# Expert tokens turned by VectorE in 32x32 blocks instead of by TensorE

## The reference, cut to what matters

```
aff = softmax(tok @ router_w)                 # (512, 16), per sequence
gate, idx = top_k(aff.T, 64)                  # per expert
xs = tok[idx]                                 # 128 slots of both sequences x 1024
hid = silu(xs @ w_gate[e]) * (xs @ w_up[e])   # 1024 -> 1408
ye = (hid @ w_down[e]) * gate                 # 1408 -> 1024
out = zeros.at[idx].add(ye)
```

## Time and profile before

| what | us |
|---|---|
| median of three runs | 1491.75 |
| span of the profiled execution, first to last instruction | 1489.4 |
| TensorE busy | 1467.0 |
| VectorE busy | 1189.5 |
| ScalarE busy | 819.8 |
| GpSimd busy | 167.3 |

### The profile page before, as it was taken

One profiled execution on the slowest core, in us unless ns is written; L12 is line 12 of the kernel. 1 busy time (PEld: TensorE's weight loads), 2 busy tenths in 40 slices (PEclk: granted clock), 3 DMA queues, 4 the chain that ended last, 5 costly groups with the idle time before them and its releaser, 6 DMA issues.

```text
span 1489.4 us, 18913 instructions
## 1 busy us (share of the span) xinstructions
PE 1467.0 (99%) x7042; PEld 1235.5 (83%) x7042; DVE 1189.5 (80%) x1024; ACT 819.8 (55%) x777; POOL 167.3 (11%) x119
## 2 busy tenths in 40 slices
PE   9999999999999999998999999999999999999996
PEld 8878888888888888888888888888888888888885
DVE  5688988896767766346888888888888888888886
ACT  6322232123622222333677777777777777777776
POOL 1000001000005200011110112011110121012101
PEclk9999999999999999999999999999999999999998
DMA  7210232623263255677999999999999999999997
GB/s 236 58 43 0 81 87 75 224 85 99 94 230 121 87 183 197 227 253 283 347 362 365 376 376 374 384 374 377 374 377 381 377 374 374 384 376 376 374 374 286
DMA packets 220971, 388.26 MB, mean 261 GB/s; under 512 B 8603, under 2 KB 87771, under 8 KB 220412
## 3 DMA queue, kind: packets, MB, share of 16 engines
q1 hardware_dynamic: 213692, 361.39, 68.4%
q0 software_dynamic: 7232, 26.22, 5.8%
HBM read 348.78 MB, written 38.80 MB: 260 GB/s over the span
## 4 chain that ended last, share of the span: by engine, by line
PE 71%; DVE 2%; DMA 0%; issue 0%; ACT 0%; POOLq 0%; POOL 0%; ACTq 0%
PE ps L1779 23%; PE ps L1781 22%; PE ps L1780 22%; PE ps L2162 1%; PE ps L2154 1%; PE ps L2199 1%; PE ps L2082 0%; PE ps L2064 0%; DMA slot_tokens<-tok_rows,rows_to_gather 0%; DVE top_index L1651 0%; DVE affinity_rows L1654 0%; DVE top_of_halves L1647 0%; DVE expert_lo L1207 0%; DVE tok_rows L1592 0%; ACT expert_hi L804 0%
## 5 line engine op out<-in xcount | busy, mean ns | idle before, releaser
L1207 DVE TENSOR_TENSOR expert_lo<-expert_raw,expert_hi 128x2048 fp32r<-128x2048 f32 (+1 forms) x285 | 597.5, 2110 | 92.1 <-ACT expert_hi L804 91.1
L804 ACT ACTIVATE expert_hi<-expert_raw 128x2048 fp32r<-128x2048 f32 (+1 forms) x285 | 506.5, 1778 | 177.8 <-PE ps L1781 174.0
L1779 PE MATMUL ps<-expert_hi,slot_tokens_T_hi 128*128 128x512 f32 (+1 forms) x768 | 289.8, 377 | 2.0 <-DVE slot_tokens_T_lo L1207 1.0
L1780 PE MATMUL ps<-expert_lo,slot_tokens_T_hi 128*128 128x512 f32 (+1 forms) x768 | 285.2, 371 | 0.0
L1781 PE MATMUL ps<-expert_hi,slot_tokens_T_lo 128*128 128x512 f32 (+1 forms) x768 | 285.2, 371 | 0.0
L1779 PE MATMUL ps<-hT_hi,w_hi 128*128 128x512 f32 x576 | 226.2, 393 | 1.0 <-DVE hT_lo L1219 1.0
L1781 PE MATMUL ps<-hT_hi,w_lo 128*128 128x512 f32 x576 | 224.3, 389 | 0.0
L1780 PE MATMUL ps<-hT_lo,w_hi 128*128 128x512 f32 x576 | 224.2, 389 | 0.0
L1779 PEld LDWEIGHTS ps<-expert_hi,slot_tokens_T_hi 128*128 128x128 f32 x768 | 144.1, 188 | 25.1 <-issue 4.0
L1781 PEld LDWEIGHTS ps<-expert_hi,slot_tokens_T_lo 128*128 128x128 f32 x768 | 144.2, 188 | 20.4
L1241 DVE SCALAR_TENSOR_TENSOR conv_sum<-a_padded,small_params,conv_sum 128x1024 f32<-128x1024 f32 x120 | 158.1, 1317 | 3.4
(11 more groups left out here) (314 smaller groups left out, 1843.6 us busy)
## 6 DMA issues: line engine op xcount, KB each, us to landing
expert_raw<-in_w_gate SPq DMA_DIRECT2D x64, 1024.0 KB, 8.7
expert_raw<-in_w_up SPq DMA_DIRECT2D x64, 1024.0 KB, 8.6
expert_raw<-in_w_down SPq DMA_DIRECT2D x64, 1024.0 KB, 8.1
expert_raw<-in_w_gate SPq DMA_DIRECT2D x32, 768.0 KB, 7.5
expert_raw<-in_w_up SPq DMA_DIRECT2D x32, 768.0 KB, 7.2
expert_raw<-in_w_down SPq DMA_DIRECT2D x32, 768.0 KB, 8.5
w_raw<-in_w_in SPq DMA_DIRECT2D x36, 512.0 KB, 4.8
gate_in<-gate_spill SPq DMA_DIRECT2D x22, 512.0 KB, 3.9
```

The costliest lines, as they stand in the source:

```text
L804: nc.scalar.activation(out, src, ACT.Copy, **scale).then_inc(s, 1)
L1207: V.tensor_tensor(out, src, high_part.bitcast(F32), ALU.subtract).then_inc(s, 1)
L1779: nc.tensor.matmul(out, a[0], b[0], start=first, stop=False)
L1780: nc.tensor.matmul(out, a[0], b[1], start=False, stop=False)
```

## The change

VectorE turns the tokens of experts 1 to 15. It transposes 32x32 blocks only, and within a group of 32 partitions. So the tokens are gathered in another order: each slot's row of 1024 channels is cut into four pieces of 256 (1 KB), and partition group b gets piece b of the slots. Column group a of `slot_tokens` (256 columns) holds slots 32a to 32a + 31. That takes four gathers per expert, with a list of pieces (4 x row + quarter) that is made once: four small ScalarE copies, four small TensorE transposes (`slot_pieces`) and one VectorE operation. Read with a step of 8 elements (32 bytes) and turned block by block, the tokens come out with channel 8p + k on partition p of tile k, so the gate and up blocks are loaded with partition p holding rows 8p + 4kh to 8p + 4kh + 3. The w_down blocks are loaded as they were.

The turning (`turn_tokens`) is one VectorE instruction of 128 x 1024 elements into a buffer of its own (`turned_tokens`), at n = 8 of the body before. The split reads this buffer, not PSUM, and stands ahead of the split of block 0 on both ScalarE and VectorE. TensorE loses the eight transposes in all bodies but for expert 0; it does `hidden_T(2)` straight behind unit 17 and waits for the tokens' low part after it. GpSimd's order is now gather(e + 1), scatter(e - 1). The row of the last norm's weights is loaded at the end, since its buffer's place is taken by `turned_tokens`.

```diff
+    tok_pieces = tok_dram.rearrange("t (b c) -> (t b) c", b=4)
...
+        XS_BY_TILE = XS[:].rearrange("p (n k) -> p k n", k=KD)
+        TURNED = at("turned_tokens", 160, [P, KD, P])
...
-            return w[bass.ds(e, 1), k * 4 * P:(k + 1) * 4 * P, a:a + n].rearrange(
-                "o (t p) n -> p (o t) n", p=P), 4, n
+            return w[bass.ds(e, 1), :, a:a + n].rearrange(
+                "o (p t) n -> p (o t) n", p=P)[:, 4 * k:4 * k + 4, :], 4, n
...
-                    sp.dma_start(NGF[:], norm_f_g.to_broadcast([P, D])).then_inc(norm_g_in, 16)
...
+            sp.wait_ge(xsT_lo, E)
+            sp.dma_start(NGF[:], norm_f_g.to_broadcast([P, D])).then_inc(norm_g_in, 16)
...
             def gather(e):
-                if not isinstance(e, int):
-                    pool.wait_ge(xs_in, e * 16)
-                    pool.wait_ge(xsT_mm, e)
-                pool.wait_ge(slots_ready, 2)
-                nc.gpsimd.tensor_copy(NEXT_ROWS[:], SLOTS[:, bass.ds(e, 1)]).then_inc(rows_next, 1)
+                pool.wait_ge(xs_in, (e - 1) * 64 + 16)
+                ge(pool, xs_turned, e)
+                pool.wait_ge(slots_ready, 5)
+                nc.gpsimd.tensor_copy(NEXT_PIECES[:], PIECES[:, bass.ds(e, 1), :].rearrange("p o a -> p (o a)")).then_inc(rows_next, 1)
...
-                pool.indirect_dma_start(XS[:], None, tok_dram,
-                                        bass.IndirectOffsetOnAxis(ap=NEXT_ROWS[:], axis=0)).then_inc(xs_in, 16)
+                for a in range(4):
+                    pool.indirect_dma_start(XS[:, a * 256:(a + 1) * 256], None, tok_pieces,
+                                            bass.IndirectOffsetOnAxis(ap=NEXT_PIECES[:, a:a + 1], axis=0)).then_inc(xs_in, 16)
...
             gather(1)
+            gather(2)
             scatter(0)
-            with pool.Fori(1, E - 1) as e:
+            with pool.Fori(2, E - 1) as e:
                 gather(e + 1)
-                scatter(e)
+                scatter(e - 1)
+            scatter(E - 2)
...
             def xsT_high(e):
-                act.wait_ge(xsT_mm, e + 1)
-                high(XST[0][:].rearrange("p k n -> p (k n)"), PS[:, 6:8, :].rearrange("p a n -> p (a n)"), xsT_hi)
+                act.wait_ge(xs_turned, e + 1)
+                act.wait_ge(e_used, e * NB - SKIPPED - len(down_units(1)))
+                high(XST[0][:].rearrange("p k n -> p (k n)"), TURNED[:].rearrange("p k n -> p (k n)"), xsT_hi)
...
             def act_body(e, base, first, last=False):
                 for n in range(NB):
+                    if n == 0 and not first:
+                        xsT_high(e)
...
+            def turn_tokens(e):
+                dve.wait_ge(xs_in, e * 64 + 16)
+                V.transpose(TURNED[:], XS_BY_TILE).then_inc(xs_turned, 1)
+
+            TURN_AT = 8
...
+                    if n == 0 and not first:
+                        xsT_low(e)
...
+                    if n == TURN_AT and not last:
+                        turn_tokens(e + 1)
...
                 else:
-                    tokens_of(e + 1)
                     down(1, e, down_counts(1, e, base))
+                    hidden_T(2, e)
                     pe.wait_ge(xsT_lo, e + 2)
-                    hidden_T(2, e)
 
             keep_busy(22)
+            slot_pieces()
             tokens_of(0)
```

More of the change, by code:

```diff
@@ L100, in hybrid_encoder_kernel @@
         HALF_START = at("half_start", 6.625, [P, 1])
+        QUARTER = at("quarter_of_partitions", 6.65625, [P, 1])
+        PIECES = at("pieces_of_slots", 4.0, [P, E, 4], U32)
+        FOUR_TIMES = at("slots_four_times", 150, [E, 4, 4, P // 4])
+        NEXT_PIECES = at("pieces_to_gather", 7.8125, [P, 4], U32)
         NORMC = at("filter_norm_column", 7.5, [P, 2 * KC])
@@ L286, in hybrid_encoder_kernel @@
         e_hi, e_lo, e_used = sem("e_hi"), sem("e_lo"), sem("e_used")
[L287 to L288 removed]
+        rows_next, xs_in, xs_turned, xsT_hi, xsT_lo = (
+            sem("rows_next"), sem("xs_in"), sem("xs_turned"), sem("xsT_hi"), sem("xsT_lo"))
         silu_ready, hid_ready, hidT_mm, hidT_hi, hidT_lo = (
@@ L741, in gather @@
             def gather(e):
-                if not isinstance(e, int):
-                    pool.wait_ge(xs_in, e * 16)
-                    pool.wait_ge(xsT_mm, e)
-                pool.wait_ge(slots_ready, 2)
-                nc.gpsimd.tensor_copy(NEXT_ROWS[:], SLOTS[:, bass.ds(e, 1)]).then_inc(rows_next, 1)
+                pool.wait_ge(xs_in, (e - 1) * 64 + 16)
+                ge(pool, xs_turned, e)
+                pool.wait_ge(slots_ready, 5)
+                nc.gpsimd.tensor_copy(NEXT_PIECES[:], PIECES[:, bass.ds(e, 1), :].rearrange("p o a -> p (o a)")).then_inc(rows_next, 1)
                 pool.wait_ge(x2_mm, WO_DONE)
                 pool.wait_ge(rows_next, e)
-                pool.indirect_dma_start(XS[:], None, tok_dram,
-                                        bass.IndirectOffsetOnAxis(ap=NEXT_ROWS[:], axis=0)).then_inc(xs_in, 16)
+                for a in range(4):
+                    pool.indirect_dma_start(XS[:, a * 256:(a + 1) * 256], None, tok_pieces,
+                                            bass.IndirectOffsetOnAxis(ap=NEXT_PIECES[:, a:a + 1], axis=0)).then_inc(xs_in, 16)
             def scatter(e):
-                if not isinstance(e, int):
+                if not (isinstance(e, int) and e == 0):
                     pool.wait_ge(added, e * 16)
@@ L1134, in act_body @@
                             nc.scalar.activation(LISTS[:, g, 0, :], TOP[32 * g:32 * g + E, :], ACT.Copy).then_inc(rows_ready, 1)
-                    if n == (2 if first else 0):
+                    if first and n == 2:
+                        act.wait_ge(pair_ready, 1)
+                        for a in range(4):
+                            part = nc.scalar.activation(FOUR_TIMES[:, a, :, :], PAIR[:, 1, 32 * a:32 * a + 32][:, None, :].to_broadcast([E, 4, P // 4]),
+                                                        ACT.Copy)
+                        part.then_inc(rows_ready, 1)
+                    if first and n == 2:
                         xsT_high(e)
@@ L1567, in _ @@
                 steps.did(V.memset(HALF_START[32 * g:32 * g + 32, :], float(H * g)))
+                steps.did(V.memset(QUARTER[32 * g:32 * g + 32, :], float(g)))
             def row_scale(t):
@@ L1713, in xsT_low @@
                         XST[0][:, 4:8, :].rearrange("p k n -> p (k n)"), xsT_lo)
+                    dve.wait_ge(slots_mm, 3)
+                    V.tensor_scalar(PIECES[:].rearrange("p e a -> p a e"), PS[:, 4, 0:4 * E].rearrange("p (a e) -> p a e", a=4),
+                                    4.0, QUARTER[:], ALU.mult, ALU.add).then_inc(slots_ready, 1)
                     return
                 dve.wait_ge(xsT_hi, e + 1)
-                low(XST[1][:].rearrange("p k n -> p (k n)"), PS[:, 6:8, :].rearrange("p a n -> p (a n)"),
+                low(XST[1][:].rearrange("p k n -> p (k n)"), TURNED[:].rearrange("p k n -> p (k n)"),
                     XST[0][:].rearrange("p k n -> p (k n)"), xsT_lo)
+            def turn_tokens(e):
+                dve.wait_ge(xs_in, e * 64 + 16)
+                V.transpose(TURNED[:], XS_BY_TILE).then_inc(xs_turned, 1)
+            TURN_AT = 8
             def dve_body(e, base, first, last=False):
                 for n in range(NB):
+                    if n == 0 and not first:
+                        xsT_low(e)
                     if not (first and LEAD <= n < LEAD + SKIPPED) and not (last and n == NB - 1):
                         split_e(n, e, base)
-                    if n == (1 if first else 0):
+                    if first and n == 1:
                         xsT_low(e)
@@ L2148, in _, with slot_pieces @@
             nc.tensor.transpose(PS[:, 0, 0:E], PAIR[:, 0, :], IDENT[0:E, 0:E]).then_inc(slots_mm, 1)
+            def slot_pieces():
+                pe.wait_ge(rows_ready, 6)
+                for a in range(4):
+                    mm = nc.tensor.transpose(PS[:, 4, a * E:(a + 1) * E], FOUR_TIMES[:, a, :, :].rearrange("e b n -> e (b n)"),
+                                             IDENT[0:E, 0:E])
+                mm.then_inc(slots_mm, 1)
             def tokens_of(e):
@@ L2153, in tokens_of @@
                 for k in range(KD):
-                    mm = nc.tensor.transpose(PS[:, 6 + k // 4, (k % 4) * P:(k % 4 + 1) * P], XS[:, k * P:(k + 1) * P], IDENT)
+                    mm = nc.tensor.transpose(PS[:, 6 + k // 4, (k % 4) * P:(k % 4 + 1) * P], XS_BY_TILE[:, k, :], IDENT)
                     if isinstance(e, int) and e == 0 and k == 3:
                         mm.then_inc(affT_mm, 1)
-                mm.then_inc(xsT_mm, 1)
+                mm.then_inc(xs_turned, 1)
             def hidden_T(c, e):
@@ L2211, in pe_body @@
                 if first:
+                    pe.wait_ge(slots_ready, 5)
                     gate_up(1, e, base, (0,))
```

13 lines of the change are left out of this document (7 added, 6 removed).

## The result

The kernel after takes 1506.7 us (median of 4 runs, 1506.4 to 1508.4) against 1491.9 before: a ratio of 1.0100, 95% interval 1.0086 to 1.0114. I had forecast 1485.7, faster; it is slower, nearest to rival B's 1501.7, and above the top of my range, 1503. The profiled execution has a span of 1505.1 us, 15.7 more than the one before.

What follows compares the result with a forecast made beforehand. TensorE was taken as the bound, VectorE and the loads close behind. Per expert -0.47, times 15 = -7.0, plus 1.0 at the start: 1489.4 to 1483.4; the median's 2.35 more gives 1485.7 us, range 1482 to 1503.

Steps and rivals of the forecast that it cites:

- rival B: VectorE's transpose takes two steps per element, 2.29 us; TensorE waits 1.13 at unit 9 of each expert: 1501.7 us; chance 0.38.
- T = 1.22: Duration in us of VectorE's new 128x1024 transpose per expert, taken from two-source passes, one with an 8-byte step.
- T - 1.16: TensorE's wait at unit 9 of each expert behind VectorE's transpose of duration T; forecast as 0.06 us.
- -0.87: TensorE's gross gain in us per expert, experts 1 to 15, from losing eight token transposes; 13.1 us in all.
- The start, 1 us: First expert: the four gathers may land after VectorE wants them at n = 8; 0 to 4 us once, 1 taken.
- cover: nobody needs them: GpSimd's four gathers, up to 10.4 us per expert, aren't needed until n = 8 of the next expert, over 40 us later.
- Unit 16, +0.34: At unit 16 of each expert TensorE waits for its weights' split, which the removed transposes had covered: 0.34 us lost.
- Block 0 with the tokens' split ahead of it: Next expert's block 0 is split after the tokens, yet ready with 0.2 us to spare; priced at 0.
- 384 packets: Extra packets of 1 KB per expert from the gathers, slowing the loads by 0.27 us per expert, 4 in all.
- The cap: The weight loads' lead at expert 15 limits what TensorE can win to 8.4 us.
- the norm's weights, priced at 0: Loading the last norm's weights at the end, behind all weight blocks, was taken to cost 0.
- Rival C: Extra packets or the new row order lengthen the loads' period by 2.0 us per expert: +17.6, 1509 us; chance 0.05.

Runs made afterwards that it cites:

- e2: Kernel after with the transpose reading slot_tokens in one contiguous piece (output not the reference's): 1496.4 us, ratio 1.0035.
- e4: Kernel after with only the first expert's turn moved from behind block 8 to behind block 12: 1502.6 us, ratio 1.0074.
- e3: Kernel before with each gather of experts 1 to 15 issued as four of a quarter of the columns, transposes still on TensorE: 1495.0 us, ratio 1.0024.
- e1: Kernel after with the turn behind block 12's split in place of block 8's, in every expert: 1492.4 us, ratio 1.0005.
- e11: Kernel of e1 with turned_tokens laid on expert_out's place and the last norm's weights loaded at the start again: 1490.7 us, ratio 0.9998.
- t1: A separate kernel without the encoder, timing VectorE's transposes, copies and subtractions by step: 1024-column transpose 2.01 us at 32 bytes, 1.25 in one piece.
- e9: Kernel before with one more 256 KB load per expert (1 to 15) behind block 9, into a buffer nobody reads: 1496.0 us, ratio 1.0025.

## Why the prediction was wrong

- **T = 1.22: the step that failed.** It measured 2.15 (2.01 without the other engines). The stall T - 1.16 was the right formula: 0.99 by it, and the period came out at 48.28, where -0.87 + 0.34 + 0.99 makes 48.25. The range of T was wide enough (0.75 to 2.29); the value was taken from the nearest row by its step of 8 bytes, and the rule that spoke against it was waved off with that very row. That row could not decide: 8 bytes is on the cheap side of both explanations. Over 14 experts the period's error is 0.96 x 14 = 13.4 us of the 21.0 that I missed by.
- **The start, 1 us: right in kind, too small.** The gather was late by 1.98, inside my 0 to 4. But the whole of T stood behind it: 1.98 + 2.15 less the slack of about 1 is the 3.04 that PE waits at unit 9. By the times, the copy of the piece list made 1.8 of the 1.98 (2.02 long beside a split of DVE, 0.19 by itself). Expert 0 lost 4.68, where my steps make +0.5. Beyond the wait that is 1.6, which the clock at 0.50 for 3.4 us behind it makes (half of the stretch); it was in no step of mine. e2 waited 2.2 at the same place, kept its clock at 1.00 there and lost 2.4 in that expert; e4 gives all of it back. There is one trace of the kernel after, so whether each execution has this drop of the clock is open.
- **GpSimd's gathers: "cover: nobody needs them".** True for the queue, as e3's unchanged period shows. The drain at the end was on no list of mine: +3.27.
- **Unit 16, +0.34: right.** PE starts it 0.05 after DVE's split in all experts. Block 0 with the tokens' split ahead of it: right, ready 0.14 before PE starts it, where I had 0.2.
- **Loads.** The pace was near (0.21 for 0.27 per expert), by luck: the 384 packets that it was worked out from are not there (48 small ones, e3). My fixed part of a row was also mixed from units of 1000 and 1024 bytes; it is 9.5 ns by my rows, not 11, which makes 0.23. The cap was right, seen in e1: TensorE won 8.4 up to expert 15, and the loads' last lead was down to 2.1. What I left out is what lies behind them in the queue: final_rows, late by 4.4, and the norm's weights, priced at 0 and worth 1.3 to 1.7 (e11). In the kernel after this is hidden, since the stall leaves the loads more lead (19.8 us for the last block that is split, 14.0 before).
- **Rival B** had the mechanism, the place and nearly the size (T 2.29 and period 48.4, measured 2.15 and 48.28). Its 1501.7 missed the 3.3 of the drain and the larger start. Rival C is what bounds the repaired kernel, at a smaller price than it had.
- The sum with every term as measured: +0.6 (not of the change), +4.7, +7.1, +3.3 = 15.7, the difference of the spans. From after to e11 16.0 us come back, the stalls of the experts and of the first one; but the 8.5 that TensorE has then won over the kernel before go to the drain (3.3) and to what the last loads delay.

## What to carry to other kernels

Work that leaves the bounding engine is worth no more than the lead of what stands next behind it, here some 8 us of loads; work that goes to another engine costs what its place has no cover for, not its share of that engine (0 at block 12, 0.99 at block 8, for the same 2.15 us). Take the price of an access pattern from a row with the same step, or from the side of the range that a stated rule points to; a row that both explanations predict alike decides nothing. And look at the program's end as at a stage: what each added DMA leaves for the last drain, and what queues behind the last loads.

## What the runs showed of the hardware that was not expected

- DVE's fp32 transpose reads at the same cost with steps of 4 and 8 bytes (446 ns for 256 columns), and at 0.74 ns more per element with steps of 16 and 32 (630 and 634). At 32 bytes, the only step tried for them, writing costs as much more (2016 against 1246 for 1024 columns), and so does one source of a subtraction (1994 against 1226). A plain copy went from 694 to 1082 ns (t1).
- GpSimd's drain at the end grows with the DMAs that it has issued: 0.18, 4.73, 5.55 and 8.00 us for 0, 52, 67 and 97. With 52 DMAs it was 4.47 in e9. Whether by steps, and whether by DMAs or by their descriptors, was not tried apart.
- GpSimd's copy of 128x4 elements takes 0.19 us alone and beside DVE's transposes (t1), and, where it meets DVE's two-source subtractions, it lasts until 0.05 behind the end of one of them: mostly of the third in a row in the kernel after (5.9 on average), of the first or second in e1, of the first in e2 (2.1 in both). So the copy waits for a subtraction, and sometimes for the next ones too; this is read from the times of the copies' ends, and no run took the subtractions away, and what decides how many it waits for is open. It cost something only in the first expert.
- TensorE's granted clock fell from 1.00 to 0.50 1.1 us after an idle stretch of 3.04 us had ended, and came back 3.4 us later (kernel after, at 737.2); behind an idle stretch of 2.2 us at the same place in e2 it stayed at 1.00.
